# Setup, projection and attention of a hybrid encoder block joined into one phase of 68 slots

## The reference

```python
h_in = rms_norm(x, norm1_w[layer]).astype(x.dtype)
z = h_in @ w_in[layer]
z_attn, z_rwkv, z_gate = jnp.split(z, cuts, axis=-1)
q = rms_norm(qkv[:, :, 0], q_norm_w[layer]) * HEAD_DIM ** -0.5
kq = rms_norm(qkv[:, :, 1], k_norm_w[layer])
...
zr = token_shift_centred(z_rwkv.astype(f32), shift_mu_prev[layer], shift_mu_next[layer])
r, k_raw, v_raw, w_lo, a_lo, g_lo = jnp.split(zr, rwkv_cuts, axis=-1)
w_log = -jax.nn.softplus(-(decay_w0[layer][:, None, None, :]
                           + jnp.einsum('bsr,zrc->zbsc', jnp.tanh(w_lo), decay_w2[layer]))) - 0.5
...
iclr = jax.nn.sigmoid(iclr_a0[layer][:, None, None, :]
                      + jnp.einsum('bsr,zrc->zbsc', a_lo, iclr_a2[layer]))
gate = jax.nn.sigmoid(g_lo) @ gate_g2[layer]
...
x = x + merged.astype(x.dtype) @ w_out[layer]
h2 = rms_norm(x, norm2_w[layer]).astype(x.dtype)
hid = jax.nn.silu(h2 @ w_ffn_gate[layer]) * (h2 @ w_ffn_up[layer])
x = x + hid @ w_ffn_down[layer]
```

## Time and profile before

| | us |
|---|---|
| median of 3 runs | 3734.99 |
| lowest, highest | 3720.21, 3741.87 |
| profiled execution | 3735.87 |
| its span | 3734.2 |

### The profile page before, as it was taken

One profiled execution on the slowest core, in us unless ns is written; L12 is line 12 of the kernel. 1 busy time (PEld: TensorE's weight loads), 2 busy tenths in 40 slices (PEclk: granted clock), 3 DMA queues, 4 the chain that ended last, 5 costly groups with the idle time before them and its releaser, 6 DMA issues.

```text
span 3734.2 us, 44512 instructions
## 1 busy us (share of the span) xinstructions
PE 3501.4 (94%) x16478; PEld 2815.9 (75%) x16478; DVE 1554.9 (42%) x1899; ACT 1092.6 (29%) x1713; POOL 1664.4 (45%) x1381
## 2 busy tenths in 40 slices
PE   5899998999988999999778899999999999999999
PEld 4277776777757888888546687888888888888887
DVE  3056641555556777776233354331233023303321
ACT  3322212444314454454232222221222122222211
POOL 2033333332326888888334443444443444444343
PEclk8599999999999999999889999999999999999999
DMA  5333343333335545544433442333333333233323
GB/s 166 121 96 110 94 120 115 113 113 112 89 104 136 130 119 137 130 116 120 143 88 101 122 120 86 99 90 93 107 92 88 103 101 95 86 103 98 101 84 107
DMA packets 765936, 406.07 MB, mean 109 GB/s; under 512 B 191774, under 2 KB 726490, under 8 KB 765306
## 3 DMA queue, kind: packets, MB, share of 16 engines
q1 hardware_dynamic: 765818, 404.53, 38.3%
HBM read 345.73 MB, written 58.72 MB: 108 GB/s over the span
## 4 chain that ended last, share of the span: by engine, by line
PE 44%; DMA 2%; DVE 2%; issue 1%; ACT 1%; SPq 0%; POOL 0%; DVEq 0%; ACTq 0%; POOLq 0%
PE f_bank L145 15%; PE f_bank L146 15%; PE f_bank L147 15%; DMA w_raw_b<-in_w_branch_attn_dram 1%; DMA w_raw_b<-in_w_branch_rwkv_dram 1%; DVE hid_plain L2246 1%; ACT w_hi_b L129 0%; POOL w_lo_b L136 0%; SPq L1891 0%; DVE hid_plain L2243 0%; ACT hid_plain L2046 0%; DMA act_plain<-yt 0%; DVE hid_plain L2200 0%; PE f_bank L1947 0%; DVE hid_plain L2310 0%
## 5 line engine op out<-in xcount | busy, mean ns | idle before, releaser
L136 POOL TENSOR_TENSOR w_lo_b<-w_raw_b,w_hi_b 128x2048 fp32r<-128x2048 f32 (+3 forms) x200 | 743.7, 3719 | 1012.7 <-ACT w_hi_b L129 1012.6
L145 PE MATMUL f_bank<-act_rounded,w_lo_b 128*128 128x512 f32 x1664 | 649.8, 390 | 23.3 <-POOL act_rounded L2161 15.5
L146 PE MATMUL f_bank<-act_rounded,w_hi_b 128*128 128x512 f32 x1664 | 649.3, 390 | 0.0
L147 PE MATMUL f_bank<-act_rounded,w_hi_b 128*128 128x512 f32 x1664 | 649.0, 390 | 0.0
L129 ACT CAST w_hi_b<-w_raw_b 128x2048 fp32r<-128x2048 f32 (+3 forms) x200 | 313.0, 1565 | 927.7 <-PE f_bank L147 858.7
L145 PEld LDWEIGHTS f_bank<-act_rounded,w_lo_b 128*128 128x128 f32 x1664 | 313.6, 188 | 89.8 <-POOL act_rounded L2161 16.0
L147 PEld LDWEIGHTS f_bank<-act_rounded,w_hi_b 128*128 128x128 f32 x1664 | 313.6, 188 | 65.3
L146 PEld LDWEIGHTS f_bank<-act_rounded,w_hi_b 128*128 128x128 f32 x1664 | 313.4, 188 | 65.1
L136 POOL TENSOR_TENSOR w_lo<-w_raw,w_hi 128x2048 fp32r<-128x2048 f32 x39 | 179.5, 4605 | 381.4 <-ACT w_hi L129 381.4
L863 POOL TENSOR_TENSOR blocks<-blocks,inv_step 32x30 f32<-32x30 f32 (+14 forms) x480 | 273.4, 570 | 37.6
L860 POOL TENSOR_TENSOR inv_step<-blocks 32x30 f32<-32x30 f32 (+14 forms) x480 | 268.4, 559 | 37.5
(11 more groups left out here) (353 smaller groups left out, 5948.0 us busy)
## 6 DMA issues: line engine op xcount, KB each, us to landing
w_raw_b<-in_w_ffn_gate_dram SPq DMA_DIRECT2D x44, 1024.0 KB, 5.2
w_raw_b<-in_w_ffn_up_dram SPq DMA_DIRECT2D x44, 1024.0 KB, 5.2
w_raw_b<-in_w_ffn_down_dram SPq DMA_DIRECT2D x64, 704.0 KB, 4.6
w_raw<-in_w_in_dram SPq DMA_DIRECT2D x39, 1024.0 KB, 5.7
slab_w_plain<-in_w_in_dram SPq DMA_DIRECT2D x58, 512.0 KB, 4.2
gate_w_plain<-in_w_in_dram SPq DMA_DIRECT2D x54, 512.0 KB, 5.0
w_raw_b<-in_w_out_dram SPq DMA_DIRECT2D x16, 1024.0 KB, 6.0
zt<-lout SPq DMA_DIRECT2D x40, 256.0 KB, 2.1
```

Of the source, the lines that this page charges most:

```text
L136: pool.tensor_tensor(g.w_lo[n.slot][:, 0:k, :], g.w_raw[n.slot][:, 0:k, :], g.w_hi[n.slot][:, 0:k, :].bitcast(F32), ALU.subtract).then_inc ...
L145: pe.matmul(bank, wl, hi[:, ka, :], start=start and j == 0, stop=False)
L146: pe.matmul(bank, wh, lo[:, ka, :], start=False, stop=False)
L147: ins = pe.matmul(bank, wh, hi[:, ka, :], start=False, stop=stop and j == len(ks) - 1)
```

## The change

`phase_setup`, the old `phase_project` and `phase_attention` become one `phase_project` of 68 slots: 3 low-rank slabs (`Q0 = 3`), 36 of q, k, v in the order q0, k0, v0, q1, ... (`A0 = 39`), 24 of r, k, v (`G0 = 63`), 5 of gates. All take half slabs from the rings of the old attention phase; the stages of a slot are written out by `pro_pe`, `pro_dve`, `pro_act`, which are the old lists with these additions:

```diff
+NORMS = [x for x in range(Q0, G0) if (x - Q0) % 3 == 1 or ((x - Q0) % 3 == 0 and x < A0)]
+JOBS_A_SLOT = 4
+def jobs_in(s):
+    i, off = divmod(s - (Q0 + 4), 3)
+    return [] if off or i < 0 else list(range(JOBS_A_SLOT * i, min(JOBS_A_SLOT * i + JOBS_A_SLOT, len(LORA_JOBS))))
+def pro_pe(s):
+    stages = [("open", s, 4 if s == A0 else 0)]
+    if s - 2 in NORMS:
+        stages.append(("heads", s - 2, 0))
+    for j in jobs_in(s):
+        stages.append(("job", j, 3))
...
+def pro_act(s):
...
+    if s - 2 in NORMS:
+        stages.append(("root", s - 2))
+    jobs = jobs_in(s)
+    stages += [("job", j) for j in jobs[:2]]
+    stages.append(("high", 2 * s + 3))
+    stages += [("job", j) for j in jobs[2:]]
...
+    if s - 1 in NORMS:
+        stages.append(("square", s - 1))
+    if s == Q0:
+        stages.append(("bend", 0))
...
+    stages.append(("high", 2 * s + 4))
```

```diff
+                for t in range(TT):
+                    sp.dma_start(x_tok[:, t, :], a["x"][0, t * P:(t + 1) * P, :]).then_inc(x_landed[t], 16)
+                    if t == 1:
+                        weights(0)
...
+                for h in range(1, 4):
+                    weights(h)
+                for dst, src in row_loads[1:]:
+                    sp.dma_start(dst, src).then_inc(rows_landed, 16)
+                for t in range(TT):
+                    sp.wait_ge(raw_taken, 4 * t + 4)
+                    sp.dma_start(xt.rearrange("(k p) n -> p k n", p=P)[:, :, t * P:(t + 1) * P], x_turned[t % 2][:, :, :]
+                                 ).then_inc(x_kept[t % 2], 16)
                 for s in range(N_SLOT + 2):
                     weights(2 * s + 4)
+                    if s == 0:
+                        for z in range(2):
+                            sp.dma_start(w2[0:64, z, :], a["decay_w2"][0, z]).then_inc(w2_landed, 16)
...
+                square_sum(0)
+                square_sum(1)
+                scale(0)
+                square_sum(2)
+                scale(1)
+                square_sum(3)
+                high(0)
+                scale(2)
+                scale(3)
+                for k in range(KD):
+                    high_h(k)
+                    if k in (3, 9):
+                        high(1 + k // 6)
...
+                def keep(t, b):
+                    dve.wait_ge(raw_turned, 4 * t + b + 1)
+                    if t >= 2:
+                        dve.wait_ge(x_kept[t % 2], 16)
+                    dve.tensor_copy(x_turned[t % 2][:, 4 * b:4 * b + 4, :].rearrange("p a n -> p (a n)"), four_banks[b]).then_inc(raw_taken, 1)
...
+                for t in range(TT):
+                    if t < 3:
+                        for b in range(4):
+                            keep(t, b)
+                            if b == 1:
+                                mean_square(t)
+                    else:
+                        mean_square(t)
+                    if t >= 1:
+                        scale(t - 1)
...
+                scale(3)
+                for k in range(KD):
+                    low_h(k)
+                    if k % 4 == 3:
+                        keep(3, k // 4)
...
+                def turn_x(k):
+                    if k >= 2:
+                        pe.wait_ge(low_ready, k - 1)
+                    for t in range(TT):
+                        if k == 0:
+                            pe.wait_ge(scaled_act, t + 1)
+                        if k == KD // 2:
+                            pe.wait_ge(scaled_dve, t + 1)
+                        ins = pe.transpose(turn_banks[k % 2][:, t * P:(t + 1) * P], x_tok[:, t, k * P:(k + 1) * P], g.ident[:, :])
+                    ins.then_inc(turned, 1)
...
+                turn_x(0)
+                turn_x(1)
+                for k in range(KD):
+                    tile(0, k)
+                    if k + 2 < KD:
+                        turn_x(k + 2)
+                pe.wait_ge(rows_landed, 16 * (len(row_loads) - 1))
+                pe.wait_ge(low_ready, KD)
+                pe.transpose(pv_ps[:, 0:P], rows_a[:, :], g.ident[:, :])
+                pe.transpose(pv_ps[:, P:2 * P], rows_b[:, :], g.ident[:, :]).then_inc(par_turned, 1)
```

More of the change, by code:

```diff
@@ L775, in phase_scan @@
         gbank = [ctx.enter_context(nc.psum_tensor(f"gbank{b}", [P, SEQ], F32)) for b in range(2)]
+        ends = sb("g_ends", [P, ROW_BYTES // 2 // (4 * NQ), NQ])
+        g_end = [ends[:, i, :] for i in range(NSET + 1)]
+        w_lo, w_raw = two_faced(nc, ctx, "gate_w", [P, RAW_RING * KH, P])
+        w_hi = sb("gate_w_hi", [P, HI_RING * KH, P], F32R)
         r_in, k_in, kk_in, sw_in, ic_in, v_in = (sb(n, [P, NQ, CH]) for n in ("r_in", "k_in", "kk_in", "sw_in", "ic_in", "v_in"))
@@ L789, in phase_scan @@
         low = [sb(f"low{s}", [P, NQ, P]) for s in S2]
-        g_end = [sb(f"g_end{i}", [P, NQ]) for i in range(NSET + 1)]
         d_bd = [sb(f"d_bd{i}", [P, NQ, P]) for i in range(2)]
@@ new lines, in taking, with finished @@
+def taking(x):
+    return "shift" if x < Q0 or A0 <= x < G0 else "take"
+def finished(x):
+    return "unit" if x in NORMS and x < A0 else taking(x)
+def pro_pe(s):
[4 more added lines that the diff above has]
+        stages.append(("job", j, 3))
+    n, m = unit_in(s), unit_in(s - 1)
+    if n is not None:
+        stages.append(("scores", n, 3))
+    if m is not None:
+        if m % ATT_PER_PAIR == 0:
+            j = m // ATT_PER_PAIR
+            stages += [("turn_v0", j, 2), ("turn_v12", j, 2)]
+        stages += [("turn_p", m, 5), ("sum", m, 0)]
+    if s == G0 + 1:
+        stages += [("turn_rows", gr, 2) for gr in range(3)]
+    if s == G0 + 3:
+        stages += [("spread", n, 2) for n in range(8)]
+    if s == G0 + 4:
+        stages += [("spread", n, 2) for n in range(8, N_BC)]
+    return stages
@@ L1424, in phase_attention @@
         sem = nc.alloc_semaphore
+        w_lo, w_raw = two_faced(nc, ctx, "slab_w", [P, RING * KH, P])
+        w_hi = sb("slab_w_hi", [P, (RING - 1) * KH, P], F32R)
+        out = [sb(f"slab_out{i}", [P, SEQ]) for i in range(NOUT)]
+        sq, floor, y, t_sb, kk_out = (sb(n, [P, SEQ]) for n in ("n_sq", "n_floor", "n_y", "n_t", "kk_out"))
+        with ExitStack() as early:
+            eb = lambda n, s, d=F32: early.enter_context(nc.sbuf_tensor(n, s, d))
+            x_tok = eb("x_tok", [P, TT, D_MODEL])
+            x_turned = [eb(f"x_turned{i}", [P, KD, P]) for i in range(2)]
+            lora = eb("lora", [P, 3, SEQ])
+            w2, g2 = eb("w2", [P, 2, RW]), eb("g2", [P, 2, RW])
+            lout = eb("lout", [P, NLOUT, SEQ])
+            rows_a, rows_b = eb("rows_a", [P, P]), eb("rows_b", [P, P])
+            ssq, ms, rstd, neg_half = (eb(n, [P, TT]) for n in ("ssq", "ms", "rstd", "neg_half"))
+        junk = lout[:, :, :].rearrange("p a n -> p (a n)")
         q_sb, k_sb, v_sb = ([sb(f"{n}{i}", [P, SEQ]) for i in range(3)] for n in ("q_sb", "k_sb", "v_sb"))
@@ L1634, in _ @@
[L1634 to L1644 removed]
+                            src, rows = bank[n % 2], P
@@ L1734, in _ @@
                     k = 0
-                    for name, n, tiles in att_pe(s):
+                    for name, n, tiles in pro_pe(s):
                         ins = None
                         if name == "heads":
-                            pe.wait_ge(taken_act, ATT_ACT_AT["square", n])
-                            if n >= 3:
-                                pe.wait_ge(taken_dve, ATT_DVE_AT["floor", n - 3])
+                            pe.wait_ge(taken_act, ACT_DONE["square", n])
+                            before = norm_before(n)
+                            if before is not None:
+                                pe.wait_ge(taken_dve, DVE_DONE["floor", before])
```

881 lines of the change are left out of this document (321 added, 560 removed).

## The result

The changed kernel takes 3645.43 us in the median (3640.23 to 3647.75, 4 runs) beside 3738.32 for the kernel before (3720.21 to 3741.87, 4 runs): a ratio of 0.9759, 95% interval [0.973, 0.9788], faster. The forecast was 3671 with a range of 3643 to 3700. So the sign and the range held, and the forecast was 26 us too high. The span of the profiled execution is 3642.6 us against a forecast of 3670.4, 27.8 less, and that is what the rest of this text accounts for.

The account below looks back on a forecast made before the run. TensorE was taken as the bound. Attention starting 61.7 us earlier (start gives 94.0, slots 3 to 38 take back 32.3) and 2.1 less by coming in warm give a span of 3670.4, forecast 3671 us, range 3643 to 3700.

Parts of the forecast that it names:

- The bound, and where the gain lies: TensorE busy 3501.4 of 3734.2 us; gain lies before attention, whose first slab starts at 576.7 instead of 638.4.
- Price of a slab, 11.25: Projection slab of 16 tiles of three matmuls: 11.25 us, read from old drains; 405.0 us for slots 3 to 38.
- Products between tiles: 40 low-rank products in slots 3 to 38, three tiles apart: 1.24 us each, 2.2 for gate products, 57.2 together.
- The first tile: Start of slot 0: first xt store lands at 28.2, VectorE's queue follows, first tile at about 36.8 us.
- Slot 0, 1.8 us a k: First slab with its transposes: 1.8 us a k between 1.45 and 2.2, 29.7 us in all, end at 66.5.
- Does a stretch of transposes get the full clock?: Slot 0's clock left open: the skill's no gives 2.2 us a k, a full-speed row can give less.
- The cold start: Rival: slot 0 stays at 1.2 GHz, slot 1 begins cold, halves 4 and 5 late; 3684 us, 3698 with dear jobs; chance 0.18.
- Slots 1 and 2: Slabs behind slot 0: 22.5 us plus 0.7 transposes, 1 stall for late half slabs, 1 cold restart; slot 3 at 91.7.
- Supply behind slot 2, and the clock in the job slots: Projection: no POOL low-half wait over 1 us behind slot 2; rivals: supply falls behind (3711 to 3731, 0.09), clock falls (0.06).
- Attention: Attention's 29 slabs keep their work but come in warm, 2.1 us less; prediction wrong if outside 453 to 456 us.
- The rest: Code behind attention, 2628.4 us behind 1105.6, and the change of phase ahead of it: the same before and after.
- The "fast start" rival: Rival: xt store lands before DVE wants the buffer, slot 0 runs warm; 3655 us, 3644 with jobs' lower bound; chance 0.12.

Follow-up runs that it names:

- The eleven variants: Follow-up kernels, each the changed kernel with tile offsets, store order, low-rank product grouping or spread timing altered, alone or combined; 3627.22 to 3661.67 us.
- the first experiment: Changed kernel with only its attention and projection weight tiles put back at the old offset, 32 bytes behind a multiple of 64; 3661.67 us, ratio 0.9803.

## Why the prediction was right, and where it was off

The result lies inside the range by 2.4 us, and below the 3657 to 3682 in which the forecast itself was to lie. With the old offset (3661.67) it would have been inside both: the mechanism was right, and one term was too dear.

*The bound, and where the gain lies*: right. PE works without a pause from 83.4 to 553.9; the low-rank slabs at 1.2 GHz are gone; 61.7 us earlier at attention's start was forecast, 84.5 came.

*Price of a slab, 11.25*: this is the step that failed by most. It was read rightly, but that "another layout of slope and g_end" costs "nothing" was wrong. Going back to the old offset costs 10.6 us in slots 3 to 38, so it carries 10.6 of the 14.5 that this stage was too dear, and 16 of the 26 by which the forecast was too high. The other 3.9 are the insertions: with the old offset three slots with two head sums and four products take 6.66 above their slabs, where 0.95 and 1.24 make 6.86; those with the gate products take 10.1 above theirs for 10.7; head sums inside a slot cost about 0.84, and only 23 of the 24 lie in these slots (that of slot 37's k stands in slot 39).

*Products between tiles*: 1.24 was right (1.14 of insertion and 0.10 on the next tile). That three tiles give their copies the time they need was the argument for it; in the run without tiles between them nothing waits, so none is needed.

*The first tile*: the chain was right, the size was 2.3 too high: the store landed at 26.4 for 28.2.

*Slot 0, 1.8 us a k*: measured 22.87 / 16 = 1.43, just under the lower bound's 1.45. But this profile had the shortest slot 0 of all. The eleven variants took 24.3 to 24.9 for it: two or three of the first tiles at 1.9 to 2.1, and the others at about 1.5. A fair size of the miss is thus 5 and not 7. The value between the two levels was the wrong choice, since the full clock for most of the slot was the rule.

*Does a stretch of transposes get the full clock?* With the first store ahead, PE did nothing but transposes up to the first tile at 30.4; its stretches 22 to 27 and 27 to 29 us, PE alone:

```profile
22.00:27.00 5.00, 3.88 (x19) 0.53 0.66 198
27.00:29.00 2.00, 0.87 (x6) 1.00 0.15 43
```

Nearly 4 us of transposes at half clock, and then the full one was granted. In the kernel before it was not: there transposes alone kept PE 73% busy from 31 to 47 us, at 0.53. The Trainium skill (TensorE: Matmul & The Clock Gate, Part 4: PE-mode transpose) says that the full clock does not engage for transposes; in this run it did, for fp32 transposes of 128 x 128, and the measurement decides. The cold start, the rival by which the loop stays at 1.2 GHz, did not come.

*Slots 1 and 2*: 26.0 for 25.2. The wait was where it was expected, 2.2 for 1, and the half clock behind it about 1.9 for 1. Taking the store out of the queue removed both.

*Supply behind slot 2, and the clock in the job slots*: as forecast. PE waits for nothing between 83.3 and 553.8, and the clock is 1.00. In this stretch no job slot is longer than 17.9 and no slot without jobs longer than 12.3, apart from those into which the first product of the next slot's group falls (12.46 and 13.32).

*Attention*: 452.1 for 453.7. The prediction called itself wrong if this stretch was not 453 to 456 us, and it lies just outside. The cause is the offset again: with the old one the stretch is 455.1. By the new offset its slots are 0.2 shorter each (6 in sum), and slot 66 is 3.1 longer, by the half clock behind the wait of 1.1. With the slower slabs of the first experiment this wait was 0.5, so a faster TensorE meets it sooner; whether the clock falls behind it differs from one execution to the next. The forecast had neither.

*The rest*: the span behind the start of slot 67 is 2651.8; behind attention's last slab of the kernel before it is 2655.3, of that kernel with aligned tiles 2657, and in the variants of after 2648 to 2654. The 3.5 us there are code that was not changed, and I did not settle them.

The range of 3643 to 3700 held, with the result near its low end. The "fast start" rival (3655, 3644 with cheap jobs) gives nearly the measured number, and half of its reasons: slot 0 ran at the full clock in this profile and was 6.8 shorter, where it had 6. But the store did not land before DVE wanted the buffer, the stalls came, and the jobs cost what was forecast. Most of the difference came from the offset, which no rival had.

## What to carry to other kernels

Before a duration is carried from an old trace to a changed kernel, look whether the change moves tiles in SBUF; for these slab matmuls, begin weight tiles at a multiple of 256 bytes in the partition and moving tiles at one of 512. Whatever gets faster meets the next wait sooner, and a wait of 1 to 3 us can cost 2 to 3 more by the clock, once 7.7. Look for the slots in which supply is just in time, and when you have moved something to help them, look whether the wait itself is gone before you credit the edit. Put small matmuls of another kind together rather than between tiles once no copy holds them back, and keep a store that waits out of the queue that brings the next weights.

## What the runs showed of the hardware that I had not expected

- The slab matmuls of 512 columns start 227 ns apart with weights at a multiple of 256 or 512 bytes and moving tiles at one of 512, 232 with weights at 128, 233 to 235 at 64 or 32, and 234 with only the moving operand off.
- Transposes alone brought the granted clock from 0.53 to 1.00 with the first store ahead; in the kernel before, a longer stretch of them stayed at 0.53.
- Behind waits of equal length (1.1 us; 2.1 to 2.2 us) the clock fell in some executions and stayed in others, and where it fell behind 1.1 us the half clock lasted some 7 us or, once, some 17.
- A change from slab matmuls to a plain fp32 product and back costs about 0.3 us, without any wait.
- DVE's scaling of half a token tile took 0.75 us and then, beside POOL's subtraction of a half slab (30.79 to 33.14), 2.69. All twelve profiles with this setup have the same pair of times; no run takes POOL's work away, so that POOL is the cause is likely and not shown. The timeline of DVE of after:

```profile
29.66 0.75 DVE L1387 TENSOR_SCALAR x_tok<-x_tok,rstd 128x1024 f32<-128x1024 f32 x1
30.99 2.69 DVE L1387 TENSOR_SCALAR x_tok<-x_tok,rstd 128x1024 f32<-128x1024 f32 x1 [0.58 <-PE pt_ps L1575]
```
